# A hybrid decoder trunk: one step of the written-out order moved by a place on TensorE (twice), VectorE and GpSimd

## The chip, the cores and the metric

One core of one Trainium2 chip runs the whole program. The metric is the device time of one execution in microseconds (us).

## What is computed

The program takes 512 tokens of width 1024 through two decoder layers, after 16 learned meta tokens have been put in front (528 tokens; the 16 are dropped at the end). A layer is

```python
a = rms_norm(h, attn_norm)
proj = a @ w_in                     # columns parted among three head groups
o_a = dsa_attention(...)            # an indexer's scores choose 128 keys of each query, then softmax
o_b = forgetting_attention(...)     # softmax with q.k + cumsum(log_f) differences
o_c = gla_chunked(...)              # gated linear attention
h = h + concat(o_a, o_b, o_c) @ w_out
f = rms_norm(h, ffn_norm)
h = h + (silu(f @ w_gate) * (f @ w_up)) @ w_down
```

The four queries and keys of the first two groups are RMS-normed over each head of 64 features. All products are float32.

## The kernel before

**Products.** A float32 product is made of three: the weight is rounded to a high part (`whi`, ScalarE, L1702), the remainder is `wlo = raw - whi` (GpSimd, L888), the activations are split likewise (`xhi`, `xlo`), and TensorE adds `whi*xhi` (L1115), `whi*xlo` (L1116) and `wlo*xhi` (L1121) in one PSUM bank.

**Input projection.** `w_in` is cut into 24 units of 128 columns: unit 6 and 7 are the FoX queries, 8 and 9 the FoX keys, 10 and 11 the FoX values. A unit's 528 tokens are two halves of 264 (query units of layer 1: one of 512). A half is one PSUM bank and three pieces on TensorE, `("proj", unit, half, piece)`: pieces 0 and 1 are eight matmuls each with `whi`, piece 2 eight matmuls with `wlo`. VectorE then evicts the bank to `feat`, times the row's 1/rms (L2251, "eviction"). Three banks go round: the half three places later in the projection's order waits on TensorE for this eviction. ScalarE's and GpSimd's step `("proj", k, 1, 2)` rounds, or makes the remainder of, unit k + 2, since a buffer of two units is kept; the remainder's count (`split_done`) releases both piece 2 of that unit and the load of unit k + 4 on the DMA queue.

**The mixers between.** Everything else of the mixers is laid between these pieces. Steps that bear on the change:

- `norm(k)`, head norm of unit k: ScalarE squares the tile (L1772, L1773), GpSimd splits the squares (`sq_parts`, L982), TensorE sums them over the head with a block of ones (L1136) into a ring of four further banks, ScalarE takes the reciprocal root (L1742, L1783), and VectorE multiplies tile by gain by root (L2261).
- `split_q(n)`: ScalarE's high part (L1799) and VectorE's remainder (L2300) of half a query tile; numbers 4 to 7 are the sparse attention's four query heads. `logits(0, i, hd)` on TensorE (L1193) waits for `split_q(4 + hd)` on VectorE, and VectorE then adds the mask and takes the minimum (L2443) and frees the bank.
- `fox_log` and `spread_sums`: the forget gate's logarithm (ScalarE), its running sum (VectorE, L2345), and four copies of it into the rows of `k_fox` (GpSimd, L955): the "gate sums".
- `gate(t)`: two matmuls of the linear attention's gate (L1181).
- `index(i, hd)`: an indexer tile (TensorE L1193; ScalarE's relu L1894; VectorE's sum L2381).
- `topk`: rounds of maximum and replacement on VectorE (L2392, L2393).

**What sets the order.** Each engine runs its own list in order. The lists are written out by hand as strings in `STEPS_OF` (L258), one string for each layer and engine; a letter is a chain of steps, and each occurrence takes the next step of that chain that the engine has a part in (`ordered`, L315). A is the projection, D the norms, X the logits, Q GpSimd's clears (`masks`, `clear_fox`, `spread_sums`, ...). Banks of the ring follow from the order of the ring's jobs on TensorE (`BANKS_OF`, `Places`). Engines meet only at semaphores, so a list decides both what an engine does next and what it stands behind. A norm's matmuls, for example, wait like this (L1124):

```python
if k in SPLIT_SQUARES:
    pe.wait_ge(ev.sq_split, SPLIT_SQUARES.index(k) + 1)
```

and the first logit tiles of the sparse attention like this (L1204):

```python
pe.wait_ge(ev.key_split, 4)
pe.wait_ge(ev.query_split, 4 + hd + 1)
```

After the mixers each layer has its output projection and feed-forward on TensorE, which the change doesn't touch.

Of the kernel before, what the change touches and what calls it, by code (L numbers as in the profile page):

```python
# [115 lines left out]
PE, ACTE, DVEE, POOLE, DMAE = "PE", "ACT", "DVE", "POOL", "DMA"  # L116
# [120 lines left out]
class Places:  # L237
# [5 lines left out]
    def take(self, job, at):  # L243
# [12 lines left out]


STEPS_OF = (  # L258
    {PE: "AAAAAAAAAAAABAAADAAAAAAAFAAAAALAAAAAAAAADAMAAMDAAMMMMMMAAMAMAAADAAAAAADAPAAAAAAAAPAAXAXAAXADXAAALAaA"
     "LAAbAdDAAAAAXAXAXXAXXAaAXAAYXYbMAXMAAAAAadMAMAZYZXYAXZYXZAYXbAAAAdZYXZAZYAAXLAPAZRAARPALYXAYAXMaAMab"  # L260
     "AAAdLZZYAXYXZZbYAXYdZAAYAZZXXYXAYALXATSRSaAAATRTRSSATTaZbYXAdZADAZYAXYXDZYXAZbAYdDZAAAAYaZDYZAXXZAAX"
     "bAYdAXAYXaZYXZYXZYXZbYadZYZYZfZbfdfff",
     ACTE: "ABCADAPALHIHACIADCIMIMDMMMMMMCAMMDAJCODIPIAJAPCXIIXDCXXALaPLADeJJXAXXXXAaXYYMMAXXXaMMYXeYYYAXPXeAYXK"
     "YLXPAPLYXYXMaaMLeYYXYXYAXeXYYXALTYXaTATXTXTCYUaeCXDYAXYDYCUDeCXXYYDYaXXAUXeYXYaUYXXYXVXYVYVYVYAeae",
     DVEE: "AAAAADAFAAAPIAHAHIADMMIIDMMMMMMAAFNADANAOANDANANIAIXNIXAXINNXDNNAANNNcNANDNNNNXXXAXXAXPXAeXPAMMMAMcN"
     "XANNPXANXNPAXcXNAePeXXNARANRXNAMMXNMMcANNeNAXXNcNXeNANXNXXNXNSSRNRNARSSANNcNXNeNANXDXNAUDXcNNeDNANND"
     "XXAcAXXeUAXUXUVXVVXcVWWWWece",
     POOLE: "AAQAQAAACACAQAACQACAAQAAAQAAAACACCCAAA",
     DMAE: "AEEEAGAAEAEAGAAAAAAAAAAAAAAAAAA"},
    {PE: "AAAAAAAAABDAAAAAAAFAAAAALAADAMMAMDAAMMMAMMAADMAMAAAADAAAAADXXAAAXAAYYXAMAAAAAMaAMAAADAAMALALAAXAAAPA"  # L270
     "PAZYZAYXAXAAAAAZAYXAAAaZYAAAXbLAZYAAXAZYXZYAXAZbYXAAMAaRAARALMAPAAPALLASTSARATRASTSdRATZYXTZYXZYAXZY"
     "bXdADAadZZYYXADXZYZbXYAXZYXaZYXZDAZYAYXdbXZYXZaZYYdXZbXYdZXYaZXYZXZYXYbDZYZYZaZdbfdffff",
     ACTE: "BCAADAAHIICLADIHMMCMAIDMMMMMCADMMCPADICIAIIDAXXOXYAYJJXMaMJCMADJMALLAPPXAPYYXXYAXaYLAXYPYXXYXKYMAaLM"
     "APPXALLTATTUeTYYTYCXXYeXACDaXeYYUXDYYXAXCaYUXYDXYCXYUXYeXaYXeYXVeYXVXaYAYXYXYXDYVYVaee",
     DVEE: "AADAAFAAAIHIDAIMMHMIDMMAMMFANMDNAADIIXIXIDXAAAXMMONMNNANMNANDNNNANANNPNXANNNNNANANAXPAXPXANAPNcPXNXX"
     "NXAPMAMAMXNNRRANMANNANNNSNNSRNNRNNScARSeNXNNXNNXXANceNXeDUNAXXDcNUXXNXNNDNAXcXUUXeVVXecXWeXVXXXcWDVW"
     "Wcee",
     POOLE: "QQAAAAAACACACAAQQCAQAAAAAAQAAAACACCAAC",
     DMAE: "AEEEAGAAEAEAGAAAAAAAAAAAAAAAAAA"},
)  # L280
# [2737 lines left out]
```

## Time and profile before

| | |
|---|---|
| three runs | 1248.36, 1248.59 (median), 1249.31 us |
| profiled execution | span 1246.9 us from first to last instruction; the median of the runs is 1.7 us more |
| TensorE busy | 1232.7 us, 99% of the span |
| VectorE, ScalarE, GpSimd busy | 1025.6, 699.0, 171.2 us |
| granted TensorE clock | 1.000 on average |

The profile is of one execution, in microseconds from the start of its span. PE is TensorE, DVE VectorE, ACT ScalarE, POOL GpSimd. A timeline row gives start and duration, and where the engine stood idle before it, how long, and what released it. A matmul's row is longer than its step to the next, since matmuls overlap. Layer 0's mixers run from the start to some 238 us, layer 1's from about 640 to 860 us.

### The profile page before, as it was taken

The page shows a single profiled execution, that of the slowest core. Times are in us where ns is not written, and L with a number is a line of the kernel's source. Part 1 is how long each engine was busy: PE and PEld are TensorE (multiplying, and loading weights), DVE is VectorE, ACT ScalarE, POOL GpSimd, SP SyncE. Part 2 cuts the span into 40 slices and gives each one's busy share as a digit, 9 for nine tenths or more (in the row PEclk, how much of TensorE's full clock was granted, in tenths as well). Part 3 has the DMA queues.
Part 4 walks back from the last instruction along what each step waited for, and adds up shares of the span by engine and source line. Part 5 has one row for each costly group of instructions (what it writes and reads, how often), then busy time and mean ns, then how long its engine had stood idle before and what let it go on. Part 6 is the DMA issues. An engine that isn't in the chain of part 4 may idle for free.

```text
span 1246.9 us, 23723 instructions
## 1 busy us (share of the span) xinstructions
PE 1232.7 (99%) x9336; PEld 1181.9 (95%) x9336; DVE 1025.6 (82%) x1692; ACT 699.0 (56%) x1158; POOL 171.2 (14%) x120
## 2 busy tenths in 40 slices
PE   7999999999999999999999999999999999999999
PEld 7999999999999999999998899988899999998998
DVE  5797789588999999897665888894989999989865
ACT  6675547656555555753355765395665555558332
POOL 2564213100000000000033553121000000000000
PEclk9999999999999999999999999999999999999999
DMA  5322111132322222233323221110422332212333
GB/s 198 103 73 86 52 35 35 35 135 71 133 103 102 102 102 69 85 100 118 105 89 102 92 85 53 52 35 18 135 102 102 129 109 102 102 69 85 119 119 119
DMA packets 27387, 114.01 MB, mean 91 GB/s; under 512 B 3472, under 2 KB 4112, under 8 KB 21904
## 3 DMA queue, kind: packets, MB, share of 16 engines
q1 hardware_dynamic: 26560, 111.45, 26.9%
q8 instruction: 73, 1.20, 0.4%
q10 hardware_dynamic: 720, 1.09, 0.2%
q14 instruction: 34, 0.28, 0.1%
HBM read 108.79 MB, written 2.10 MB: 89 GB/s over the span
## 4 chain that ended last, share of the span: by engine, by line
PE 94%; DVE 3%; ACT 1%; issue 1%; POOL 1%; DMA 0%; SPq 0%; DVEq 0%; ACTq 0%; POOLq 0%
PE ps L1404 22%; PE ps L1410 11%; PE ps L1019 11%; PE ps L1115 6%; PE ps L1121 6%; PE ps L1116 6%; PE ps L1025 5%; PE ps L1488 5%; PE ps L1524 4%; PE ps L1245 3%; PE ps L1493 2%; PE ps L1529 2%; PE ps L1193 2%; PE ps L1218 2%; PE ps L1228 1%
## 5 line engine op out<-in xcount | busy, mean ns | idle before, releaser
L1115 PE MATMUL ps<-xhi,whi 128*128 128x264 f32 (+1 forms) x616 | 174.0, 310 | 1.3 <-DVE feat L2251 1.3
L1116 PE MATMUL ps<-xlo,whi 128*128 128x264 f32 (+1 forms) x616 | 167.5, 300 | 0.0
L888 POOL TENSOR_TENSOR wlo<-raw,whi 128x1024 fp32r<-128x1024 f32 x48 | 119.1, 2483 | 181.6 <-ACT whi L1702 181.0
L1115 PEld LDWEIGHTS ps<-xhi,whi 128*128 128x128 f32 x616 | 116.1, 188 | 5.9 <-DVE feat L2251 1.5
L1116 PEld LDWEIGHTS ps<-xlo,whi 128*128 128x128 f32 x616 | 116.2, 189 | 3.6
L1702 ACT ACTIVATE whi<-raw 128x1024 fp32r<-128x1024 f32 x74 | 77.9, 1054 | 55.0 <-PE ps L1025 30.6
L1121 PE MATMUL ps<-xhi,wlo 128*128 128x264 f32 (+1 forms) x616 | 100.5, 305 | 0.8 <-POOL wlo L888 0.8
L1121 PEld LDWEIGHTS ps<-xhi,wlo 128*128 128x128 f32 x616 | 85.3, 188 | 5.1 <-POOL wlo L888 1.2
L1404 PE MATMUL ps<-fhi,hi_a 128*128 128x264 f32 (+1 forms) x352 | 88.2, 283 | 0.0
L1404 PE MATMUL ps<-flo,hi_a 128*128 128x264 f32 (+1 forms) x352 | 88.1, 282 | 0.0
L1404 PE MATMUL ps<-flo,hi_b 128*128 128x264 f32 (+1 forms) x320 | 80.3, 283 | 0.0
L1404 PE MATMUL ps<-fhi,hi_b 128*128 128x264 f32 (+1 forms) x320 | 80.2, 282 | 0.0
L2027 ACT ACTIVATE w_part<-ps 128x264 f32<-128x264 f32 (+1 forms) x42 | 16.3, 387 | 91.1 <-PE ps L1410 91.1
L2138 ACT ACTIVATE whi<-raw 128x1024 fp32r<-128x1024 f32 (+2 forms) x42 | 38.4, 913 | 50.5 <-PE ps L1493 29.8
L1404 PE MATMUL ps<-xlo,hi_a 128*128 128x264 f32 (+1 forms) x264 | 66.5, 284 | 0.0
L1404 PE MATMUL ps<-xhi,hi_a 128*128 128x264 f32 (+1 forms) x264 | 66.3, 283 | 0.0
L1404 PEld LDWEIGHTS ps<-flo,hi_a 128*128 128x128 f32 x352 | 66.3, 188 | 0.0
L1404 PEld LDWEIGHTS ps<-fhi,hi_a 128*128 128x128 f32 x352 | 66.2, 188 | 0.0
L2251 DVE TENSOR_TENSOR feat<-ps,rstd 128x264 f32<-128x264 f32 (+1 forms) x84 | 38.4, 466 | 26.7 <-PE ps L1121 17.2
L1404 PEld LDWEIGHTS ps<-fhi,hi_b 128*128 128x128 f32 x320 | 60.3, 188 | 0.0
L2027 ACT ACTIVATE s<-ps 128x264 f32<-128x264 f32 (+1 forms) x84 | 32.5, 387 | 49.5 <-PE ps L1410 49.5
L1404 PEld LDWEIGHTS ps<-flo,hi_b 128*128 128x128 f32 x320 | 60.3, 188 | 0.0
(376 smaller groups left out, 3871.9 us busy)
## 6 DMA issues: line engine op xcount, KB each, us to landing
raw<-in_weights SPq DMA_DIRECT2D x116, 512.0 KB, 3.5
raw<-in_groups SPq DMA_DIRECT2D x42, 1024.0 KB, 4.8
out_hT<-h SPq DMA_DIRECT2D x7, 256.0 KB, 4.9
h<-in_hT SPq DMA_DIRECT2D x4, 264.0 KB, 6.3
h<-in_hT ACTq DMA_DIRECT2D x4, 264.0 KB, 6.0
cst<-in_consts SPq DMA_DIRECT2D x1, 780.5 KB, 9.0
xnb<-feat SPq DMA_DIRECT2D x10, 66.5 KB, 2.1
feat<-xnb SPq DMA_DIRECT2D x10, 66.5 KB, 2.1
```

The costliest lines, as they stand in the source:

```text
L888: nc.gpsimd.tensor_tensor(wlo[:, b], raw[:, b], whi[:, b].bitcast(F32), ALU.subtract).then_inc(split_done, 1)
L1019: nc.tensor.matmul(bank(bank_no, cut.stop - cut.start), whi[:, b, k % KT], x(k)[t][:, cut], start=(first and k == ks[0] and t == 0), stop= ...
L1025: ins = nc.tensor.matmul(bank(bank_no, cut.stop - cut.start), wlo[:, b, k % KT], x(k)[0][:, cut], start=False, stop=(last and k == ks[-1]))
L1115: nc.tensor.matmul(o, whi[:, k % 2, n], xhi[:, n, cut], start=(n == 0), stop=False)
L1116: nc.tensor.matmul(o, whi[:, k % 2, n], xlo[:, n, cut], start=False, stop=False)
L1121: ins = nc.tensor.matmul(o, wlo[:, k % 2, n], xhi[:, n, cut], start=False, stop=(n == KT - 1))
L1404: nc.tensor.matmul(bank(bank_no, width), high[:, of], x(i)[t], start=(begins and i == 0 and t == 0), stop=False, skip_group_check=True)
L1410: ins = nc.tensor.matmul(bank(bank_no, width), low, x, start=False, stop=(n == PAIRS - 1), skip_group_check=True)
L1488: nc.tensor.matmul(to, whi[:, slot, k], hidden_tiles(k0 + k)[t][:, cut], start=(begins and k == 0 and t == 0), stop=False, skip_group_chec ...
L1524: nc.tensor.matmul(down_bank(l, bank_no), high(i), x(i)[t], start=(begins and i == 0 and t == 0), stop=False, skip_group_check=True)
L1702: return nc.scalar.activation(whi[:, b], raw[:, b], ACT.Copy).then_inc(hi_done, 1)
L2027: nc.scalar.activation(to, bank(group_banks(n)[bank_name], width), ACT.Copy).then_inc(sv.snapped, 1)
```

## The change

Four letters move by a place or three; nothing else changes (further lines of the diff only shift the indentation of the strings). No instruction is added or taken away, and the order of the ring's jobs stays, so the banks do too.

| layer, engine | before | after |
|---|---|---|
| 0, TensorE | `norm 7`, `proj 8,1,2`, `gate 0` | `proj 8,1,2`, `norm 7`, `gate 0` |
| 0, GpSimd | `spread_sums`, remainder of unit 10, remainder of unit 11 | remainder of unit 10, `spread_sums`, remainder of unit 11 |
| 1, TensorE | `proj 9,1,0`, `norm 8`, `logits 0,1,0`, `logits 0,1,1`, `proj 9,1,1`, `proj 9,1,2` | `proj 9,1,0`, `proj 9,1,1`, `norm 8`, `logits 0,1,0`, `logits 0,1,1`, `proj 9,1,2` |
| 1, VectorE | `split_q 7`, `norm 8`, `logits 0,1,2`, eviction of 9,0, eviction of 9,1 | `split_q 7`, eviction of 9,0, `norm 8`, `logits 0,1,2`, eviction of 9,1 |

```diff
 STEPS_OF = (
-    {PE: "AAAAAAAAAAAABAAADAAAAAAAFAAAAALAAAAAAAAADAMAAMDAAMMMMMMAAMAMAAADAAAAAADAPAAAAAAAAPAAXAXAAXADXAAALAaA"
+    {PE: "AAAAAAAAAAAABAAADAAAAAAAFAAAAALAAAAAAAAADAMAAMDAAMMMMMMAAMAMAAADAAAAAAADPAAAAAAAAPAAXAXAAXADXAAALAaA"
...
-     POOLE: "AAQAQAAACACAQAACQACAAQAAAQAAAACACCCAAA",
+     POOLE: "AAQAQAAACACAAQACQACAAQAAAQAAAACACCCAAA",
...
-    {PE: "AAAAAAAAABDAAAAAAAFAAAAALAADAMMAMDAAMMMAMMAADMAMAAAADAAAAADXXAAAXAAYYXAMAAAAAMaAMAAADAAMALALAAXAAAPA"
+    {PE: "AAAAAAAAABDAAAAAAAFAAAAALAADAMMAMDAAMMMAMMAADMAMAAAADAAAAAADXXAAXAAYYXAMAAAAAMaAMAAADAAMALALAAXAAAPA"
...
-     DVEE: "AADAAFAAAIHIDAIMMHMIDMMAMMFANMDNAADIIXIXIDXAAAXMMONMNNANMNANDNNNANANNPNXANNNNNANANAXPAXPXANAPNcPXNXX"
+     DVEE: "AADAAFAAAIHIDAIMMHMIDMMAMMFANMDNAADIIXIXIADXAAXMMONMNNANMNANDNNNANANNPNXANNNNNANANAXPAXPXANAPNcPXNXX"
```

## Rows read from the trace of the kernel before

**Rows 1.** The page, part 1: busy time, share of the span and instructions by engine.

```profile
PE 1232.7 (99%) x9336; PEld 1181.9 (95%) x9336; DVE 1025.6 (82%) x1692; ACT 699.0 (56%) x1158; POOL 171.2 (14%) x120
```

**Rows 2.** The waits of TensorE: line, releaser, us in total, times, longest.

```profile
PE ps L1115 <- DVE feat L2251: 1.3, 1, 1.3
PE ps L1121 <- POOL wlo L888: 0.8, 1, 0.8
```

**Rows 3.** Timeline, layer 0, TensorE: start, duration, line, tiles, count, [idle before, releaser].

```profile
69.67 0.28 PE L1116 MATMUL ps<-xlo,whi 128*128 128x264 f32 x1
70.03 0.73 PE L1136 MATMUL ps<-sq_parts,ones_r 128*128 128x266 f32 x4
70.60 1.15 PE L1121 MATMUL ps<-xhi,wlo 128*128 128x264 f32 x8
71.58 0.41 PE L1181 MATMUL ps<-lr_parts,w_parts 80*128 80x266 f32 x2
...
80.82 1.24 PE L1121 MATMUL ps<-xhi,wlo 128*128 128x264 f32 x8 [0.75 <-POOL wlo L888]
...
82.86 0.20 PE L1193 MATMUL ps<-kk,mix_hi 128*16 128x16 f32 x2
...
84.31 0.20 PE L1193 MATMUL ps<-kk,q_tables 128*16 128x16 f32 x2 [0.17 <-DVE q_tables L2300]
```

**Rows 4.** Timeline, layer 0, GpSimd.

```profile
68.54 1.34 POOL L982 TENSOR_TENSOR sq_parts<-sqb,sq_parts 128x532 fp32r<-128x532 f32 x1 [2.76 <-ACT sq_parts L1773]
...
75.19 3.12 POOL L955 COPY k_fox<-feat 4x532 f32<-4x532 f32 x4 [2.89 <-DVE feat L2345]
78.39 5.20 POOL L888 TENSOR_TENSOR wlo<-raw,whi 128x1024 fp32r<-128x1024 f32 x2
```

**Rows 5.** Timeline, layer 0, ScalarE.

```profile
71.31 0.70 ACT L1742 ACTIVATE rnb<-ps,cst 128x532 f32<-128x532 f32 x1
...
74.51 1.06 ACT L1702 ACTIVATE whi<-raw 128x1024 fp32r<-128x1024 f32 x1
...
77.91 1.06 ACT L1702 ACTIVATE whi<-raw 128x1024 fp32r<-128x1024 f32 x1
```

**Rows 6.** Timeline, layer 0, VectorE.

```profile
76.36 0.77 DVE L2261 SCALAR_TENSOR_TENSOR feat<-feat,par_all,rnb 128x532 f32<-128x532 f32 x1
...
79.88 1.45 DVE L2300 TENSOR_TENSOR mix_hi<-feat,mix_hi 64x528 fp32r<-64x528 f32 x1
...
82.55 1.61 DVE L2300 TENSOR_TENSOR q_tables<-feat,q_tables 64x528 fp32r<-64x528 f32 x1
```

**Rows 7.** Timeline, layer 1, TensorE.

```profile
702.22 0.28 PE L1116 MATMUL ps<-xlo,whi 128*128 128x264 f32 x1
702.88 0.75 PE L1136 MATMUL ps<-sq_parts,ones_r 128*128 128x266 f32 x4 [0.38 <-POOL sq_parts L982]
...
710.92 0.39 PE L1115 MATMUL ps<-xhi,whi 128*128 128x264 f32 x1 [1.33 <-DVE feat L2251]
...
712.01 0.53 PE L1193 MATMUL ps<-kk,mix_hi 128*128 128x400 f32 x2
```

**Rows 8.** Timeline, layer 1, VectorE.

```profile
707.24 2.93 DVE L2261 SCALAR_TENSOR_TENSOR feat<-feat,par_all,rnb 128x532 f32<-128x532 f32 x1
710.20 0.31 DVE L2443 CUSTOM_DVE_ANT_0 probs<-ps,score 128x144 f32<-128x144 f32 x1
...
710.44 1.11 DVE L2251 TENSOR_TENSOR feat<-ps,rstd 128x264 f32<-128x264 f32 x3
```

**Rows 9.** Timeline, layer 1, GpSimd.

```profile
707.21 2.39 POOL L888 TENSOR_TENSOR wlo<-raw,whi 128x1024 fp32r<-128x1024 f32 x1 [1.65 <-ACT whi L1702]
```

**Rows 10.** Timeline, the start, TensorE.

```profile
6.92 0.59 PE L1019 MATMUL ps<-xhi,whi 128*128 128x264 f32 x1 [6.92 <-ACT whi L1702]
...
11.59 0.42 PE L1019 MATMUL ps<-xhi,whi 128*128 128x264 f32 x1
11.81 0.42 PE L1019 MATMUL ps<-xlo,whi 128*128 128x264 f32 x1
```

More of the change, by code:

```diff
@@ L258 @@
 STEPS_OF = (
-    {PE: "AAAAAAAAAAAABAAADAAAAAAAFAAAAALAAAAAAAAADAMAAMDAAMMMMMMAAMAMAAADAAAAAADAPAAAAAAAAPAAXAXAAXADXAAALAaA"
-     "LAAbAdDAAAAAXAXAXXAXXAaAXAAYXYbMAXMAAAAAadMAMAZYZXYAXZYXZAYXbAAAAdZYXZAZYAAXLAPAZRAARPALYXAYAXMaAMab"
-     "AAAdLZZYAXYXZZbYAXYdZAAYAZZXXYXAYALXATSRSaAAATRTRSSATTaZbYXAdZADAZYAXYXDZYXAZbAYdDZAAAAYaZDYZAXXZAAX"
-     "bAYdAXAYXaZYXZYXZYXZbYadZYZYZfZbfdfff",
+    {PE: "AAAAAAAAAAAABAAADAAAAAAAFAAAAALAAAAAAAAADAMAAMDAAMMMMMMAAMAMAAADAAAAAAADPAAAAAAAAPAAXAXAAXADXAAALAaA"
+         "LAAbAdDAAAAAXAXAXXAXXAaAXAAYXYbMAXMAAAAAadMAMAZYZXYAXZYXZAYXbAAAAdZYXZAZYAAXLAPAZRAARPALYXAYAXMaAMab"
+         "AAAdLZZYAXYXZZbYAXYdZAAYAZZXXYXAYALXATSRSaAAATRTRSSATTaZbYXAdZADAZYAXYXDZYXAZbAYdDZAAAAYaZDYZAXXZAAX"
+         "bAYdAXAYXaZYXZYXZYXZbYadZYZYZfZbfdfff",
@@ L263 @@
      ACTE: "ABCADAPALHIHACIADCIMIMDMMMMMMCAMMDAJCODIPIAJAPCXIIXDCXXALaPLADeJJXAXXXXAaXYYMMAXXXaMMYXeYYYAXPXeAYXK"
-     "YLXPAPLYXYXMaaMLeYYXYXYAXeXYYXALTYXaTATXTXTCYUaeCXDYAXYDYCUDeCXXYYDYaXXAUXeYXYaUYXXYXVXYVYVYVYAeae",
+           "YLXPAPLYXYXMaaMLeYYXYXYAXeXYYXALTYXaTATXTXTCYUaeCXDYAXYDYCUDeCXXYYDYaXXAUXeYXYaUYXXYXVXYVYVYVYAeae",
      DVEE: "AAAAADAFAAAPIAHAHIADMMIIDMMMMMMAAFNADANAOANDANANIAIXNIXAXINNXDNNAANNNcNANDNNNNXXXAXXAXPXAeXPAMMMAMcN"
-     "XANNPXANXNPAXcXNAePeXXNARANRXNAMMXNMMcANNeNAXXNcNXeNANXNXXNXNSSRNRNARSSANNcNXNeNANXDXNAUDXcNNeDNANND"
@@ L267 @@
-     "XXAcAXXeUAXUXUVXVVXcVWWWWece",
-     POOLE: "AAQAQAAACACAQAACQACAAQAAAQAAAACACCCAAA",
+           "XANNPXANXNPAXcXNAePeXXNARANRXNAMMXNMMcANNeNAXXNcNXeNANXNXXNXNSSRNRNARSSANNcNXNeNANXDXNAUDXcNNeDNANND"
+           "XXAcAXXeUAXUXUVXVVXcVWWWWece",
+     POOLE: "AAQAQAAACACAAQACQACAAQAAAQAAAACACCCAAA",
      DMAE: "AEEEAGAAEAEAGAAAAAAAAAAAAAAAAAA"},
-    {PE: "AAAAAAAAABDAAAAAAAFAAAAALAADAMMAMDAAMMMAMMAADMAMAAAADAAAAADXXAAAXAAYYXAMAAAAAMaAMAAADAAMALALAAXAAAPA"
-     "PAZYZAYXAXAAAAAZAYXAAAaZYAAAXbLAZYAAXAZYXZYAXAZbYXAAMAaRAARALMAPAAPALLASTSARATRASTSdRATZYXTZYXZYAXZY"
-     "bXdADAadZZYYXADXZYZbXYAXZYXaZYXZDAZYAYXdbXZYXZaZYYdXZbXYdZXYaZXYZXZYXYbDZYZYZaZdbfdffff",
+    {PE: "AAAAAAAAABDAAAAAAAFAAAAALAADAMMAMDAAMMMAMMAADMAMAAAADAAAAAADXXAAXAAYYXAMAAAAAMaAMAAADAAMALALAAXAAAPA"
+         "PAZYZAYXAXAAAAAZAYXAAAaZYAAAXbLAZYAAXAZYXZYAXAZbYXAAMAaRAARALMAPAAPALLASTSARATRASTSdRATZYXTZYXZYAXZY"
+         "bXdADAadZZYYXADXZYZbXYAXZYXaZYXZDAZYAYXdbXZYXZaZYYdXZbXYdZXYaZXYZXZYXYbDZYZYZaZdbfdffff",
@@ L273 @@
      ACTE: "BCAADAAHIICLADIHMMCMAIDMMMMMCADMMCPADICIAIIDAXXOXYAYJJXMaMJCMADJMALLAPPXAPYYXXYAXaYLAXYPYXXYXKYMAaLM"
-     "APPXALLTATTUeTYYTYCXXYeXACDaXeYYUXDYYXAXCaYUXYDXYCXYUXYeXaYXeYXVeYXVXaYAYXYXYXDYVYVaee",
-     DVEE: "AADAAFAAAIHIDAIMMHMIDMMAMMFANMDNAADIIXIXIDXAAAXMMONMNNANMNANDNNNANANNPNXANNNNNANANAXPAXPXANAPNcPXNXX"
-     "NXAPMAMAMXNNRRANMANNANNNSNNSRNNRNNScARSeNXNNXNNXXANceNXeDUNAXXDcNUXXNXNNDNAXcXUUXeVVXecXWeXVXXXcWDVW"
-     "Wcee",
+           "APPXALLTATTUeTYYTYCXXYeXACDaXeYYUXDYYXAXCaYUXYDXYCXYUXYeXaYXeYXVeYXVXaYAYXYXYXDYVYVaee",
@@ L278 @@
+     DVEE: "AADAAFAAAIHIDAIMMHMIDMMAMMFANMDNAADIIXIXIADXAAXMMONMNNANMNANDNNNANANNPNXANNNNNANANAXPAXPXANAPNcPXNXX"
+           "NXAPMAMAMXNNRRANMANNANNNSNNSRNNRNNScARSeNXNNXNNXXANceNXeDUNAXXDcNUXXNXNNDNAXcXUUXeVVXecXWeXVXXXcWDVW"
+           "Wcee",
      POOLE: "QQAAAAAACACACAAQQCAQAAAAAAQAAAACACCAAC",
```

## The prediction, made before the changed kernel was run

> **What bounds the kernel now.** First the page's busy shares: TensorE is busy 99% of the span, VectorE 82% [rows 1]. So the sum is about TensorE's gaps alone: whatever is taken from a gap there is gained at the end, and whatever is added is lost, as no later stretch has slack to take it up. Then the waits of TensorE: after the wait at the start, its two longest are 1.3 us for an eviction and 0.8 us for a weight's remainder [rows 2], one in each place that the change touches. Then the timelines of those two places, engine by engine, for what each gap waits on and, above all, for what is next in line once it closes. The largest that could be hoped for is the sum of the gaps, some 3 us or 0.24%; 0.2% (2.5 us) is about what a measurement of this kernel can tell from no change.
>
> **Layer 0, TensorE.** Pieces of eight matmuls take 0.98 us (70.60 to 71.58), a step of 0.12. The last matmul before norm 7 starts at 69.67, so the norm could follow at 69.79; it starts at 70.03, when its squares are split (GpSimd, 68.54 + 1.34 = 69.88) [rows 3, 4]. With the piece put ahead, it fills that gap: 0.24 gained, and the norm's sums start at 69.79 + 0.98 = 70.77, ending 0.73 later at 71.50.
>
> **Layer 0, GpSimd.** The remainder of unit 10 now goes ahead of the gate sums, which took 75.19 to 78.31. Before, it ended at 80.8 and TensorE waited 0.75 for it [rows 3, 4]. It needs its rounding, which ended at 74.51 + 1.06 = 75.57. ScalarE is busy on norm 7 from 71.31 [rows 5]; that norm's sums now end at 71.50, and I take 0.1 from there to ScalarE, so all up to this rounding moves 0.29 later. It ends at 75.86, and GpSimd starts at about 76.0 (0.07 to 0.15 behind the rounding: 707.21 in layer 1). With 2.39 for a remainder [rows 9] it ends at 78.4, and TensorE wants it at 80.82 - 0.75 - 0.24 = 79.8. That wait goes: 0.75, with 0.24 together 1.0 us.
>
> **What is late next in layer 0.** In layer 1 VectorE's norm multiply L2261 is issued at 707.24, just behind a remainder of GpSimd that started at 707.21. It takes 2.93 in place of 0.77 and ends at 710.17, which is 0.57 after GpSimd (709.60) [rows 6, 8, 9]. So of the two, the one that starts second stands until the other is done. In layer 0 norm 7's multiply is at 76.36 and met no remainder before; now it falls 0.36 behind the start of unit 10's. It ends at 78.4 + 0.57 = 78.97 instead of 77.13: 1.84 late. VectorE goes in order, and so do the evictions and the two rounds of top-k behind it; the remainder of query head 0 (L2300, 79.88) comes at 81.72 [rows 6].
>
> The Trainium skill, page "SBUF — State Buffer", section "Who interferes with whom", has this as a rule: a VectorE instruction with two SBUF inputs and a GpSimd instruction that reads SBUF shut each other out, and the first keeps the ports for the whole instruction. By its word "fully blocks" the multiply would start only at GpSimd's end and take its 0.77, 0.20 more than the row's 0.57. Three such ends follow one another below, so by the rule's word the sum would be 0.6 worse. I go by the row.
>
> GpSimd meanwhile: gate sums from 78.5 for about 3.1 (one of the four copies held up by the multiply, as before), to 81.6, then the remainder of unit 11. That unit's rounding (77.91, behind norm 7's multiply on ScalarE's list) moves 1.84 too and ends at 80.8, in time [rows 4, 5]. So at 81.6 to 81.7 GpSimd's remainder and VectorE's query remainder meet, each able to hold the other.
>
> - GpSimd first, the likelier, as it leads by up to 0.1 and a lead of 0.03 was enough at 707.21: head 0's remainder ends at 81.6 + 2.39 + 0.57 = 84.56. TensorE's first logit tile needs it and goes 0.15 later (from 82.55 + 1.61 = 84.16 to 84.31 in the rows), at 84.7 instead of 82.86; it stands some 3 us. Next GpSimd's squares L982 (1.34) slip in and end at 85.8, so head 1's remainder ends at 86.35 and the second tile starts at 86.5 instead of 84.31 [rows 3, 4, 6]: **2.2 us lost**, the 1.0 of gain eaten in it.
> - VectorE first: head 0 is through at 82.4, unit 11's remainder runs from 82.3 to 84.7, head 1's ends at 85.3 and the second tile starts at 85.4: 1.1 us lost.
>
> Behind that, TensorE, VectorE and GpSimd are all shifted alike. The gate sums are wanted only by the second group's logits, many pieces later; the loads on the DMA queue hang on the remainders, unit 12's moves forward with unit 10's, unit 13's hardly moves, and neither is read for several pieces. Nothing for these.
>
> **Layer 1, TensorE.** Norm 8 could start at 702.22 + 0.12 = 702.34 and starts at 702.88 [rows 7]: the piece put ahead fills 0.54. ScalarE and GpSimd behind the norm are bound by other work there, so 0.54 is gained at the start of the next piece.
>
> **Layer 1, VectorE.** The eviction of 9,0 came behind norm 8's multiply (to 710.17) and the logit tile (710.20), at 710.5, and TensorE stood 1.33 to 710.92 for it [rows 7, 8]. Ahead of the norm it is done at 707.6, while TensorE wants the bank at 709.05. So 1.33 goes. The multiply then starts at 707.6, still behind the same remainder, and ends at the same 710.17; the logit tile still frees its bank at 710.51, and indexer tile (3,2) takes this bank. It came 1.09 behind 710.92, now at 709.05 + 1.09 = 710.14, and so waits until about 710.56: 0.42 back. Sum 0.54 + 1.33 - 0.42 = **1.45 gained**. Unit 12's remainder, some 12 us on, has its gate sums and squares moved by 0.3 to 1.4 only, which can cost 0 to 0.25; I take 1.4. Evictions of 9,1 and 10,0 keep their time or come earlier.
>
> **Sum.** 2.2 lost, 1.4 gained: 0.8 slower. The profiled span is 1246.9, which becomes 1247.7; the median of the runs stands 1.7 over the span, so 1249.4.
>
> **Rivals.**
> - *VectorE wins the meeting* at 81.7. For it: my starts are good to about 0.1 only. 1.1 - 1.4 = -0.3: 1248.3. Within 0.2% like the forecast.
> - *The multiply is not shut out*: unit 10's remainder starts after 76.36, so GpSimd waits for the multiply (0.77) and not it for GpSimd. The remainder ends at 79.5, still in time, and everything hoped for comes: layer 0 gains 1.0, layer 1 gains 1.4, 1246.2. Against it: the rounding would have to be 0.35 later than I have it. The change not doing what it says, in that the piece ahead fills nothing, is part of this only in name: lists are followed in order, so I give that none.
> - *TensorE slows after its stand* (slower). In the first case it stands 3 us at the first logit tile. At the start it stands 6.92 and then runs with a step of 0.22 instead of 0.12 [rows 3, 10], to 11.81 at least (about 5 us), which is what the lower of the two levels (1.2 against 2.4 GHz) would look like, though the mean granted clock of the whole span is given as 1.000. The price is 5 / 0.22 = 23 matmuls at 0.10: 2.3 us, so 0.8 + 2.3 = 3.1 slower, 1251.7. Against it: after the 1.33 at 710.92 the step is the usual one (1.09 for eight matmuls and their start [rows 7]); no row stands 3 us in the middle, so it decides from somewhere between 1.33 and 6.92. The Trainium skill, page "TensorE: Matmul & The Clock Gate", section "Why this matters for your kernels", warns of TensorE gaps between bursts in the middle of a kernel for this; the trace bears it out only for the start.
>
> **Chances.** Forecast (GpSimd first) 0.53, VectorE first 0.22, not shut out 0.12, slower clock 0.07, anything else 0.06. Faster by over 0.2% needs all the hoped gain and a little more than 2.4, half of "not shut out" and some of the rest: 0.09. Slower by over 0.2% needs the clock, or a further collision in layer 0 (the copies of the clears against heads 2 and 3, at most 0.3) with layer 1's gain missing: 0.12. Within 0.2%: 0.79. The range takes in the first two cases with 0.3 to 0.6 for their bounds and the spread of the runs (0.95): 1247.4 to 1250.8. It leaves out the cases at either end.
>
> **What would show it.** Right: no wait of TensorE for `wlo` near 80 and none for `feat` near 709; in their place TensorE waiting at L1193 for VectorE's L2300 (`mix_hi`, then `q_tables`) at 82 to 86 for some 3 us and 0.7; L2261 at 76.4 taking about 2.6; a wait of 0.4 at the indexer tile near 710. VectorE first: 1 us and then 1.7 at L1193. Wrong: L2261 at 0.77 there, no wait at L1193, and TensorE's gaps in layer 0 shorter than before; or matmuls with a step of 0.22 behind the stand.

## The result, and the profile after

The changed kernel takes 1250.94 us (median of 15 runs, 1250.58 to 1252.04) against 1248.65 (15 runs, 1248.2 to 1249.56): a ratio of 1.0019, 95% interval 1.0012 to 1.0026. It is 2.3 us slower; the forecast was 0.8 us slower. Its profiled execution spans 1249.1 us and took 1250.89.

First the page's busy times and the waits of TensorE, as in [rows 1, 2].

```profile
PE 1234.6 (99%) x9336; PEld 1183.7 (95%) x9336; DVE 1028.4 (82%) x1692; ACT 699.1 (56%) x1158; POOL 171.1 (14%) x120
```

```profile
PE ps L1193 <- DVE mix_hi L2300: 2.8, 1, 2.8
...
PE ps L1193 <- DVE stat L2443: 0.4, 1, 0.4
```

Both waits of [rows 2] are gone, 2.1 us together. One of 2.8 us at the first logit tile of layer 0 stands in their place, and a small one in layer 1. But the waits do not tell it all: TensorE is also *busy* 1.9 us longer with the same 9336 matmuls, so something made matmuls slower. Next the timeline of TensorE, at the start, in layer 0, in layer 1 and at the end, and the rows of before that the forecast did not need, for comparison (before first, then after).

```profile
24.44 1.14 PE L1121 MATMUL ps<-xhi,wlo 128*128 128x264 f32 x8
...
88.07 1.21 PE L1121 MATMUL ps<-xhi,wlo 128*128 128x264 f32 x8
...
716.28 1.14 PE L1121 MATMUL ps<-xhi,wlo 128*128 128x264 f32 x8
...
1242.70 1.10 PE L1493 MATMUL ps<-hhi,wlo 128*128 128x256 f32 x8
```

```profile
24.77 1.15 PE L1121 MATMUL ps<-xhi,wlo 128*128 128x264 f32 x8
...
79.94 1.13 PE L1121 MATMUL ps<-xhi,wlo 128*128 128x264 f32 x8
...
84.88 0.20 PE L1193 MATMUL ps<-kk,mix_hi 128*16 128x16 f32 x2 [2.84 <-DVE mix_hi L2300]
...
85.24 0.42 PE L1116 MATMUL ps<-xlo,whi 128*128 128x264 f32 x1
85.46 0.42 PE L1115 MATMUL ps<-xhi,whi 128*128 128x264 f32 x1
...
86.78 0.24 PE L1193 MATMUL ps<-kk,q_tables 128*16 128x16 f32 x2
86.87 1.92 PE L1121 MATMUL ps<-xhi,wlo 128*128 128x264 f32 x8
88.63 0.28 PE L1115 MATMUL ps<-xhi,whi 128*128 128x264 f32 x1
88.75 0.29 PE L1116 MATMUL ps<-xlo,whi 128*128 128x264 f32 x1
...
91.26 1.23 PE L1121 MATMUL ps<-xhi,wlo 128*128 128x264 f32 x8
...
713.71 0.63 PE L1193 MATMUL ps<-kk,mix_hi 128*128 128x400 f32 x2 [0.41 <-DVE stat L2443]
...
718.10 1.14 PE L1121 MATMUL ps<-xhi,wlo 128*128 128x264 f32 x8
...
1244.91 1.10 PE L1493 MATMUL ps<-hhi,wlo 128*128 128x256 f32 x8
```

The same matmuls, after less before: +0.33 at 24.77 (nothing has changed yet there; the start differs so from execution to execution), +3.19 at 91.26, +1.82 at 718.10, +2.21 at 1244.91. (Right ahead of the change, at 66.84 before and 67.22 after, the shift is 0.38, so what follows is good to about 0.05.) So **layer 0 lost 2.86, layer 1 gained 1.37 and gave 0.39 of it back further down** (0.98 net), and the change is worth +1.88 in these two executions. In layer 0 the stand is 2.84 long and the second tile comes at 86.78, which is 2.14 later than [rows 3] once the start's 0.33 is taken off. From there to 91.26 another 0.72 goes: between 85.24 and 88.63 matmuls of 264 columns take steps of 0.22, and 0.12 again from 88.63 on. The stretches of 1 us show why (columns: length of the stretch, busy time and instructions of TensorE, its weight loads, VectorE, ScalarE, GpSimd, then the granted TensorE clock, then DMA):

```profile
84.00:85.00 1.00, 0.12 (x3) 0.15 (x3) 0.97 (x2) 0.00 (x0) 1.00 (x2) 1.00 0.00 0
85.00:86.00 1.00, 1.00 (x7) 1.00 (x6) 0.97 (x2) 0.00 (x0) 0.92 (x1) 0.50 0.81 98
86.00:87.00 1.00, 1.00 (x8) 0.92 (x7) 0.97 (x4) 0.28 (x2) 0.97 (x1) 0.50 0.97 393
87.00:88.00 1.00, 1.00 (x6) 1.00 (x6) 0.89 (x4) 0.98 (x3) 0.88 (x3) 0.50 0.09 33
88.00:89.00 1.00, 1.00 (x9) 1.00 (x8) 0.71 (x4) 0.53 (x2) 0.85 (x1) 0.79 0.00 0
89.00:90.00 1.00, 1.00 (x12) 0.98 (x11) 0.42 (x3) 0.00 (x0) 0.00 (x0) 1.00 0.07 16
```

The granted clock, 1.00 through the stand, is 0.50 (the lower of its two levels, 1.2 GHz) from 85 to 88 and part of 88 to 89: 3 x 0.50 + 0.21 = 1.71 us of clock are missing. Before, the same stretches all read 1.00.

What VectorE and GpSimd did (their timelines, VectorE first):

```profile
76.74 2.46 DVE L2261 SCALAR_TENSOR_TENSOR feat<-feat,par_all,rnb 128x532 f32<-128x532 f32 x1
...
81.95 2.79 DVE L2300 TENSOR_TENSOR mix_hi<-feat,mix_hi 64x528 fp32r<-64x528 f32 x1
...
85.23 1.25 DVE L2300 TENSOR_TENSOR q_tables<-feat,q_tables 64x528 fp32r<-64x528 f32 x1
...
710.43 0.43 DVE L2251 TENSOR_TENSOR feat<-ps,rstd 128x264 f32<-128x264 f32 x1
710.78 2.52 DVE L2261 SCALAR_TENSOR_TENSOR feat<-feat,par_all,rnb 128x532 f32<-128x532 f32 x1
```

```profile
76.23 2.40 POOL L888 TENSOR_TENSOR wlo<-raw,whi 128x1024 fp32r<-128x1024 f32 x1 [3.54 <-ACT whi L1702]
78.69 3.06 POOL L955 COPY k_fox<-feat 4x532 f32<-4x532 f32 x4
81.83 2.34 POOL L888 TENSOR_TENSOR wlo<-raw,whi 128x1024 fp32r<-128x1024 f32 x1
...
718.23 2.92 POOL L955 COPY k_fox<-feat 4x532 f32<-4x532 f32 x4 [5.50 <-DVE feat L2345]
...
723.64 1.34 POOL L982 TENSOR_TENSOR sq_parts<-sqb,sq_parts 128x532 fp32r<-128x532 f32 x1
724.93 2.76 POOL L888 TENSOR_TENSOR wlo<-raw,whi 128x1024 fp32r<-128x1024 f32 x1
```

Unit 10's remainder starts at 76.23 and norm 7's multiply at 76.74, where it takes 2.46 for the 0.77 of [rows 6]. Then the remainder of unit 11 starts at 81.83 and head 0's remainder 0.12 later: it takes 2.79 and ends at 84.74, 0.57 after GpSimd (84.17). That is the forecast's chain on these two engines, to 0.2 us (less the start's shift) at every link. No semaphore stands between the two: the multiply was issued and its inputs were there. So engines do not meet at semaphores alone, as the description of the lists has it; VectorE and GpSimd also hold each other up directly, and no list shows that.

### The profile page after: what moved, and what is told of

Read it like the earlier page. It is cut to its first block, busy times and chain, and to the rows that moved or that the text cites. A ratio compares the mean times of both kernels' runs of the same rounds, so it can differ in the third digit from the quotient of the medians.

```text
span 1249.1 us, 23723 instructions
## 1 busy us (share of the span) xinstructions
PE 1234.6 (99%) x9336; PEld 1183.7 (95%) x9336; DVE 1028.4 (82%) x1692; ACT 699.1 (56%) x1158; POOL 171.1 (14%) x120
## 4 chain that ended last, share of the span: by engine, by line
PE 96%; DVE 3%; issue 1%; DMA 0%; ACT 0%; SPq 0%; DVEq 0%; ACTq 0%
PE ps L1404 22%; PE ps L1410 11%; PE ps L1019 11%; PE ps L1115 6%; PE ps L1121 6%; PE ps L1116 6%; PE ps L1025 5%; PE ps L1488 5%; PE ps L1524 4%; PE ps L1245 3%; PE ps L1493 2%; PE ps L1529 2%; PE ps L1193 2%; PE ps L1218 2%; PE ps L1228 1%; PE ps L1302 1%
```

## The experiments

Kernels that ran together share the runs of the kernel before: 28 runs (median 1248.47) beside `l0_only`, `l1_only`, `norm_first` and `query_first`, 33 (1248.51) beside `l0_pe_only`, `l0_pool_only`, `filled` and `tiles_later`, 27 (1248.44) beside `combined`, `l1_dve_only` and `l1_pe_only`. Diffs are against the kernel before where one part of the change is tried, else against the changed kernel. The clock is the mean granted one of an execution; all runs of the kernel before have 1.000.

### Layer 0 alone, layer 1 alone

`l0_only`:

```diff
-{PE: "AAAAAAAAAAAABAAADAAAAAAAFAAAAALAAAAAAAAADAMAAMDAAMMMMMMAAMAMAAADAAAAAADAPAAAAAAAAPAAXAXAAXADXAAALAaA"
+{PE: "AAAAAAAAAAAABAAADAAAAAAAFAAAAALAAAAAAAAADAMAAMDAAMMMMMMAAMAMAAADAAAAAAADPAAAAAAAAPAAXAXAAXADXAAALAaA"
...
-POOLE: "AAQAQAAACACAQAACQACAAQAAAQAAAACACCCAAA",
+POOLE: "AAQAQAAACACAAQACQACAAQAAAQAAAACACCCAAA",
```

> Layer 0's two moves alone, layer 1 as before. Theory (unit 10's remainder shuts out norm 7's multiply, the query remainder comes late, TensorE stands 2.8 us at the first logit tile and then runs at half the clock for some 3.4 us): 2.6 to 3.0 us slower than before, a granted clock of 0.5 behind the stand, mean clock under 1. Rival (layer 0 is harmless, the loss is in layer 1): within 0.4 us of before. Rival (the stand costs, the low clock is chance): 1.9 us slower with a clock of 1.000 in some looks.

Measured: 1251.93 (6 runs, 1251.45 to 1253.23), ratio 1.0031 (1.0019 to 1.0043): 3.5 slower, more than the 2.6 to 3.0 that were expected. Its profile has the stand of 2.84 at the first tile, and every one of its runs has a clock of 0.997 to 0.999. The six runs fall in two groups: three with 0.999 took 1251.45 to 1251.65, three with 0.997 took 1252.2 to 1253.23, and the profiled one is of the first group.

`l1_only`:

```diff
-{PE: "AAAAAAAAABDAAAAAAAFAAAAALAADAMMAMDAAMMMAMMAADMAMAAAADAAAAADXXAAAXAAYYXAMAAAAAMaAMAAADAAMALALAAXAAAPA"
+{PE: "AAAAAAAAABDAAAAAAAFAAAAALAADAMMAMDAAMMMAMMAADMAMAAAADAAAAAADXXAAXAAYYXAMAAAAAMaAMAAADAAMALALAAXAAAPA"
...
-DVEE: "AADAAFAAAIHIDAIMMHMIDMMAMMFANMDNAADIIXIXIDXAAAXMMONMNNANMNANDNNNANANNPNXANNNNNANANAXPAXPXANAPNcPXNXX"
+DVEE: "AADAAFAAAIHIDAIMMHMIDMMAMMFANMDNAADIIXIXIADXAAXMMONMNNANMNANDNNNANANNPNXANNNNNANANAXPAXPXANAPNcPXNXX"
```

> Layer 1's two moves alone, layer 0 as before. Theory: 0.9 us faster (1.4 gained by the twelfth projection unit, 0.4 of it given back there), clock 1.000, a wait of 0.4 at the indexer tile. Rival (layer 1 gives all of it back, or is the loss): no change, or slower.

Measured: 1247.84 (11 runs, 1246.84 to 1248.72), ratio 0.9996 (0.9987 to 1.0005), clock 1.000 in all. By its timeline, less the 0.11 that it is ahead before layer 1's change, 1.39 is gained at the piece behind the eviction and 0.98 at the end. The medians give 0.6, with an interval that takes in no change; the sign rests on the timeline. So the loss is layer 0's alone, and what layer 1 brings does not cover it.

### Which move of layer 0

`l0_pe_only`:

```diff
-{PE: "AAAAAAAAAAAABAAADAAAAAAAFAAAAALAAAAAAAAADAMAAMDAAMMMMMMAAMAMAAADAAAAAADAPAAAAAAAAPAAXAXAAXADXAAALAaA"
+{PE: "AAAAAAAAAAAABAAADAAAAAAAFAAAAALAAAAAAAAADAMAAMDAAMMMMMMAAMAMAAADAAAAAAADPAAAAAAAAPAAXAXAAXADXAAALAaA"
```

> Layer 0's move on TensorE alone: norm 7 one piece later, GpSimd in the order of before. Theory: 0.24 gained ahead of the norm and lost again at the wait for unit 10's remainder, which grows from 0.75 to 1.0; no change, within 0.2 us. Rival (the norm's delay is what makes the multiply late): slower by 1 us or more, with a stand at the logit tile.

Measured: 1248.53 (11 runs, 1248.08 to 1249.14), ratio 0.9999 (0.999 to 1.0008), clock 1.000. The 0.24 gained ahead of the norm is lost again at the weight's remainder, whose wait grows from 0.75 [rows 3] to 1.11.

`l0_pool_only`:

```diff
-POOLE: "AAQAQAAACACAQAACQACAAQAAAQAAAACACCCAAA",
+POOLE: "AAQAQAAACACAAQACQACAAQAAAQAAAACACCCAAA",
```

> Layer 0's move on GpSimd alone: unit 10's remainder ahead of the gate sums, the norm on TensorE where it was. Theory (this move alone makes the collision): the multiply of norm 7 takes 2.3, the first logit tile stands about 2.3 us, the clock falls in some runs; 2.0 to 2.8 us slower than before. Rival (it needs the norm's delay too): the multiply takes 0.77 and the kernel is 0.5 to 1 us faster than before.

Measured: 1251.34 (11 runs, 1249.86 to 1252.0), ratio 1.0021 (1.0012 to 1.003): 2.8 slower, with a stand of 2.31 and a multiply of 2.25. The clock is 0.998 or 0.999 in nine runs; the two at 1.000 took 1249.86 and 1250.19, the nine 1251.15 to 1252.0. GpSimd's move does the damage alone.

### Undoing the collision

`norm_first`: norm 7's multiply goes ahead of a round of top-k on VectorE, so that it starts before the remainder.

```diff
-DVEE: "AAAAADAFAAAPIAHAHIADMMIIDMMMMMMAAFNADANAOANDANANIAIXNIXAXINNXDNNAANNNcNANDNNNNXXXAXXAXPXAeXPAMMMAMcN"
+DVEE: "AAAAADAFAAAPIAHAHIADMMIIDMMMMMMAAFNADANAOADNANANIAIXNIXAXINNXDNNAANNNcNANDNNNNXXXAXXAXPXAeXPAMMMAMcN"
```

> The whole change, and in layer 0 VectorE does norm 7's multiply ahead of a round of top-k instead of behind it. Theory: the multiply then starts ahead of unit 10's remainder and takes its 0.77; the first logit tile waits 0.3 us at most; the second may still wait for unit 11's remainder, until about 84.4; no low clock. Layer 0 is between 0 and 1.6 us faster than before, with layer 1 in all 0.9 to 2.5 faster than before. Rival (the late gate sums or the late unit 11 are the loss, not the multiply): a stand of over 2 us at the first tile again, and 2 us slower.

Measured: 1246.40 (11 runs, 1246.22 to 1247.36), ratio 0.9985 (0.9976 to 0.9994), clock 1.000. **It is faster than both kernels**, 4.5 us below the changed one. Its timelines of VectorE, GpSimd and TensorE:

```profile
74.97 0.77 DVE L2261 SCALAR_TENSOR_TENSOR feat<-feat,par_all,rnb 128x532 f32<-128x532 f32 x1
...
79.50 1.12 DVE L2300 TENSOR_TENSOR mix_hi<-feat,mix_hi 64x528 fp32r<-64x528 f32 x1
...
81.11 0.70 DVE L2300 TENSOR_TENSOR q_tables<-feat,q_tables 64x528 fp32r<-64x528 f32 x1
```

```profile
75.47 2.53 POOL L888 TENSOR_TENSOR wlo<-raw,whi 128x1024 fp32r<-128x1024 f32 x1 [3.54 <-ACT whi L1702]
...
81.20 2.88 POOL L888 TENSOR_TENSOR wlo<-raw,whi 128x1024 fp32r<-128x1024 f32 x1
```

```profile
81.11 0.20 PE L1193 MATMUL ps<-kk,mix_hi 128*16 128x16 f32 x2
...
82.22 0.20 PE L1193 MATMUL ps<-kk,q_tables 128*16 128x16 f32 x2
...
84.79 0.20 PE L1193 MATMUL ps<-kk,mix_lo 128*16 128x16 f32 x2 [0.32 <-DVE mix_lo L2300]
```

Now the multiply is first, by 0.50, and takes its 0.77; the remainder behind it takes 2.53. At 81.11 head 1's remainder leads GpSimd by 0.09, takes its 0.70, and this time GpSimd is the one that pays (2.88 for 2.40). TensorE waits at neither of the first two tiles. So one letter in one list turns the loss into the gain that was hoped for, and the cause of the stand is that multiply's place.

`query_first`: the multiply stays where it is, but head 0's remainder goes ahead of a round of top-k.

```diff
-DVEE: "AAAAADAFAAAPIAHAHIADMMIIDMMMMMMAAFNADANAOANDANANIAIXNIXAXINNXDNNAANNNcNANDNNNNXXXAXXAXPXAeXPAMMMAMcN"
+DVEE: "AAAAADAFAAAPIAHAHIADMMIIDMMMMMMAAFNADANAOANDANAINAIXNIXAXINNXDNNAANNNcNANDNNNNXXXAXXAXPXAeXPAMMMAMcN"
```

> The whole change, and in layer 0 VectorE takes the first query remainder ahead of a round of top-k. Theory: the multiply is still shut out (some 2.4 us), but the query remainder now starts ahead of unit 11's remainder; the first tile waits under 0.6 us, the second some 2 us, until 84.7. If the clock falls only behind a stand as long as 2.8 us, it stays at 1.000, layer 0 loses 0.4 and the whole is 0.5 faster than before. Rival (the clock falls behind any stand of some 2 us): mean clock under 1, and some 1 us slower than that.

Measured: 1248.79 (11 runs, 1247.95 to 1249.78), ratio 1.0002 (0.9993 to 1.0011); 0.3 slower where 0.5 faster was expected. Head 0 is clear of the remainder (0.70), but head 1 is not: 1.98, and a stand of 2.21 at the second tile. Eight runs have a clock of 1.000 (1247.95 to 1248.89, middle 1248.58), three 0.998 or 0.999 (1249.48 to 1249.78). Those eight are level with before too, so the clock is not the whole miss: the second collision was priced too low. In the profile the second tile comes at 84.83, which is 0.71 later than [rows 3] with the start's shift of 0.19 put back, where a loss of 0.4 was expected. That is half of the 0.6 by which the eight miss; the rest is not placed.

`combined`: `norm_first`, with heads 0 and 1 ahead of a round of top-k as well (head 1 ahead of an eviction too).

```diff
-DVEE: "AAAAADAFAAAPIAHAHIADMMIIDMMMMMMAAFNADANAOANDANANIAIXNIXAXINNXDNNAANNNcNANDNNNNXXXAXXAXPXAeXPAMMMAMcN"
+DVEE: "AAAAADAFAAAPIAHAHIADMMIIDMMMMMMAAFNADANAOADNANAIINAXNIXAXINNXDNNAANNNcNANDNNNNXXXAXXAXPXAeXPAMMMAMcN"
```

> The changed kernel with norm 7's multiply ahead of a round of top-k (as in norm_first) and also head 0's and head 1's remainders ahead of one. My theory: norm_first has already taken every wait of TensorE for these tiles but 0.3 at the third, so that this gives 1246.4 within 0.3, clock 1.000. Rival: remainders that come earlier meet another GpSimd operation (the gate sums' copies) and hold it, and the remainder of unit 11 with it: a wait for wlo, 0.5 or more slower than norm_first.

Measured: 1246.26 (11 runs, 1245.91 to 1247.14), ratio 0.9983 (0.9974 to 0.9992). Level with `norm_first`, as expected. The rival's meeting is there (the gate sums' copies take 3.49 against 3.05 in `norm_first`), but TensorE does not wait for it.

### What the stand costs beside its length

`filled`: TensorE is kept at work in place of standing. Twenty matmuls are added ahead of the first tile, in its bank; the tile then overwrites what they leave. (Three lines are added, so line numbers below them are 3 higher.)

```diff
+if l == 0 and (i, hd) == (0, 0):
+    for _ in range(20):
+        nc.tensor.matmul(bank(b0, CUT), ones_r[:, 0:128], kk[:, 0, 0:CUT], start=True, stop=True)
```

> The whole change; ahead of layer 0's first logit tile TensorE runs 20 matmuls of 264 columns into the tile's own bank, about 2.4 us, which the tile then overwrites. Everything is as late as in the changed kernel, only TensorE no longer stands for 2.8 us but for 0.4. Theory (the stand costs 1.9 us in layer 0 by lateness, and what comes on top of it is the clock that falls behind it): mean clock 1.000 in every run, the second tile waits some 0.6, and the time is 1.0 us over before, 0.9 to 1.3 us under the changed kernel. Rival (the slower matmuls have another cause than the stand): clock under 1 again, and the time of the changed kernel.

Measured: 1249.75 (11 runs, 1249.02 to 1250.12), ratio 1.0006 (0.9997 to 1.0015), clock 1.000 in all eleven. TensorE's timeline:

```profile
24.66 1.14 PE L1121 MATMUL ps<-xhi,wlo 128*128 128x264 f32 x8
...
81.72 2.60 PE L1212 MATMUL ps<-kk,ones_r 128*128 128x264 f32 x20
84.68 0.21 PE L1193 MATMUL ps<-kk,mix_hi 128*16 128x16 f32 x2 [0.37 <-DVE mix_hi L2303]
...
86.52 0.20 PE L1193 MATMUL ps<-kk,q_tables 128*16 128x16 f32 x2 [0.54 <-DVE q_tables L2303]
...
90.26 1.23 PE L1121 MATMUL ps<-xhi,wlo 128*128 128x264 f32 x8
```

The remainders collide as in the changed kernel and the tiles come hardly sooner (84.68 and 86.52 against 84.88 and 86.78, of which 0.11 is the start), yet the matmuls run at full step, and 1.05 us of the loss are gone (1.24 slower than its runs of before, not 2.29; the slowest of its runs is under the fastest of the changed kernel, 1250.58). The matmul that came at 91.26 is at 90.26 here: 2.19 behind the 88.07 of before, 1.97 less the start's 0.22. So layer 0's 2.86 is **1.97 for the collisions and 0.89 for the clock** by the two timelines; by the medians the clock's share is 1.05. It is less than the 1.71 of missing clock, in the main because TensorE would have waited for the second tile anyway (0.54 here).

`tiles_later`: the four logit tiles and norm 8 go one to three pieces later on TensorE, for whom the late tiles then do not matter.

```diff
-{PE: "AAAAAAAAAAAABAAADAAAAAAAFAAAAALAAAAAAAAADAMAAMDAAMMMMMMAAMAMAAADAAAAAAADPAAAAAAAAPAAXAXAAXADXAAALAaA"
+{PE: "AAAAAAAAAAAABAAADAAAAAAAFAAAAALAAAAAAAAADAMAAMDAAMMMMMMAAMAMAAADAAAAAAADPAAAAAAAAPAAAAAXAXAXADXALAaA"
```

> The whole change, and on TensorE layer 0's four first logit tiles and norm 8 come one to three pieces later, so that pieces of the projection fill the stand. VectorE and GpSimd collide as before. Theory: the first tile waits 0.3 at most, the second 0.7, the third 0.8; no low clock; layer 0 is 0.3 faster than before, in all 1.3 faster than before (0.4 to 1.7). Rival (the lateness of the remainders is paid further down, by a wait of the later tiles or of the banks): the wait turns up behind the moved tiles and the time is that of the changed kernel.

Measured: 1248.87 (11 runs, 1248.35 to 1249.88), ratio 1.0002 (0.9993 to 1.0011), clock 1.000. Against the expectation of 1.3 faster this is a miss. The first tile no longer waits and the clock stays up, but new waits come up: 0.5 and 0.6 at the next two tiles, 0.7 for a weight's rounding, 0.5 for a softmax tile of ScalarE. Of the 2.29 of loss 1.9 are saved (0.36 slower than its runs of before): the clock's share and some 0.9 of the stand, but the lateness of VectorE is passed on to whoever needs it next, and nothing is left of layer 0's gain.

### The two moves of layer 1

`l1_dve_only`:

```diff
-DVEE: "AADAAFAAAIHIDAIMMHMIDMMAMMFANMDNAADIIXIXIDXAAAXMMONMNNANMNANDNNNANANNPNXANNNNNANANAXPAXPXANAPNcPXNXX"
+DVEE: "AADAAFAAAIHIDAIMMHMIDMMAMMFANMDNAADIIXIXIADXAAXMMONMNNANMNANDNNNANANNPNXANNNNNANANAXPAXPXANAPNcPXNXX"
```

> Layer 1's VectorE move alone: the eviction of 9,0 goes ahead of norm 8, TensorE's order stays as before, so norm 8's sums still wait for their squares. My theory: the wait of 1.33 for the eviction goes, the indexer tile gives back about 0.4 and unit 12's chain a part of the rest: 1.0 to 1.3 faster at the start of the next piece, 0.6 to 1.0 faster at the end (1247.5 to 1247.9 beside 1248.5), clock 1.000. Rival (the two moves of layer 1 need each other): without TensorE's move the time stands on norm 8 instead, and less than 0.4 is left.

Measured: 1247.88 (11 runs, 1247.14 to 1248.45), ratio 0.9995 (0.9986 to 1.0004), clock 1.000. By its timeline, less the 0.53 that it is ahead before layer 1's change, 1.35 is gained behind the eviction and 0.96 at the end: all of what `l1_only` has.

`l1_pe_only`:

```diff
-{PE: "AAAAAAAAABDAAAAAAAFAAAAALAADAMMAMDAAMMMAMMAADMAMAAAADAAAAADXXAAAXAAYYXAMAAAAAMaAMAAADAAMALALAAXAAAPA"
+{PE: "AAAAAAAAABDAAAAAAAFAAAAALAADAMMAMDAAMMMAMMAADMAMAAAADAAAAAADXXAAXAAYYXAMAAAAAMaAMAAADAAMALALAAXAAAPA"
```

> Layer 1's TensorE move alone: the piece of 9,1 fills the 0.54 ahead of norm 8, but the eviction of 9,0 still stands behind norm 8's multiply on VectorE, which ends when GpSimd's remainder ends. My theory: the wait for the eviction grows from 1.33 to about 1.9 and the time stays, within 0.2 of before, clock 1.000. Rival (the gap filled ahead of the norm is a gain of its own): 0.5 faster.

Measured: 1249.97 (11 runs, 1248.03 to 1250.56), ratio 1.0008 (0.9999 to 1.0017): 1.5 slower by the medians, with an interval that only just takes in no change, where none was expected. The first matmul behind the eviction, and the stretches of 1 us behind it (columns as above, the granted clock third from the end):

```profile
710.66 0.39 PE L1115 MATMUL ps<-xhi,whi 128*128 128x264 f32 x1 [1.78 <-DVE feat L2251]
```

```profile
711.00:712.00 1.00, 1.00 (x8) 1.00 (x7) 0.90 (x4) 0.53 (x3) 0.00 (x0) 0.69 0.89 356
712.00:713.00 1.00, 1.00 (x6) 0.99 (x5) 0.93 (x3) 0.00 (x0) 0.00 (x0) 0.50 0.20 78
713.00:714.00 1.00, 1.00 (x6) 1.00 (x6) 0.96 (x2) 0.00 (x0) 0.00 (x0) 0.50 0.00 0
714.00:715.00 1.00, 1.00 (x7) 1.00 (x7) 0.97 (x2) 0.00 (x0) 0.00 (x0) 0.60 0.00 0
```

The wait grew as expected, to 1.78, and then the clock falls, for 0.31 + 0.50 + 0.50 + 0.40 = 1.71 us as in the changed kernel. Eight runs have a clock below 1 (1249.62 to 1250.56, middle 1250.04), the other three 1248.03, 1248.09 and 1249.13. So the clock falls in a layer and behind a wait that have nothing to do with the first case: the stand does it, not what the logit tiles are. And here little of it is hidden: the matmul behind the stand comes at 710.66 against 710.92 before, but the piece of 716.28 at 717.52, so 1.50 of the 1.71 are lost there.

## Why the prediction was wrong

**Where it was right.** The likeliest case came about, link by link as far as the first logit tile. The piece ahead of norm 7 and the earlier remainder took away TensorE's waits. Norm 7's multiply fell behind unit 10's remainder and took 2.46 (forecast about 2.6). GpSimd won the meeting near 81.7, by 0.12. The first tile came 0.15 earlier than forecast and the second 0.05 earlier (84.88 and 86.78, less 0.33, against 84.7 and 86.5). For the second tile that is luck. The forecast had TensorE wait some 0.7 there, and the trace shows no wait: TensorE came to it late by itself, at the lower clock. In `filled`, at the full clock, the wait is 0.54 and the tile comes at 86.52 less 0.22, which is 0.2 earlier than forecast. The wait named for layer 1 appeared: 0.41 against 0.42 at the indexer tile. As for the Trainium skill, page "SBUF — State Buffer", section "Who interferes with whom": the runs agree that whoever is first keeps the other out, in both directions (`norm_first`), but the one kept out ends 0.57 after the other and not its full 0.70 or 0.77 later, twice more in the trace (79.20 behind 78.63, 84.74 behind 84.17). The row was the better guide. The page's "fully blocks" is said of VectorE's 2-port modes; of an instruction with two SBUF inputs, as here, it says that it contends. And what the prediction made of the rule was too much: 0.20 for each of three ends, 0.6, where the two query remainders (0.70 alone) would have come 0.13 later each, so 0.46.

**The step that failed: the sum had nothing for the clock, which had been made a rival with a chance of 0.07, and it fell in every run.** The argument against it was that "no row stands 3 us in the middle, so it decides from somewhere between 1.33 and 6.92." The forecast itself put the stand at some 3 us, well into that open stretch, and the mean clock of 1.000 was no argument: nothing in the middle of that kernel had stood so long, and the column does not cover the start, where it reads 1.00 from 7 to 12 us while matmuls take steps of 0.22 [rows 10]. The slow step behind the start's stand was the better sign. An even chance would have been fair. Put together, the longest stand in the middle (of the profiled execution; the others have no trace) against the clock:

| kernel | stand, us | runs with a clock below 1 |
|---|---|---|
| before; `l0_pe_only` | 1.33 | 0 of 15, 28, 33 and 27; 0 of 11 |
| `l1_pe_only` | 1.78 | 8 of 11 |
| `query_first` | 2.21 | 3 of 11 |
| `l0_pool_only` | 2.31 | 9 of 11 |
| after; `l0_only` | 2.84 | 15 of 15; 6 of 6 |
| `norm_first`, `combined`, `filled`, `tiles_later`, `l1_only`, `l1_dve_only` | below 1.33 | 0 of 11 each |

In these runs the first clock below 1 is met between 1.33 and 1.78. The middle of the table does not follow the length (8 of 11 at 1.78, 3 of 11 at 2.21). With eleven runs each that may be chance; whether something else decides as well was not tried and stays open. The Trainium skill, page "TensorE: Matmul & The Clock Gate", section "Why this matters for your kernels", warns of TensorE gaps between bursts in the middle of a kernel. These runs agree that such gaps cost the clock, but they show it behind shorter ones than the page sets as its bound: 1.78 us was enough in 8 of 11 runs.

**The price of that rival was off as well.** It took 5 us at the lower level from the start, 23 matmuls, 2.3 us. The stretch measured 3.4 us (85.24 to 88.63), and part of it lies in the wait for the second tile, so that it cost 0.89 by the timelines and 1.05 by the medians. So the rival's 1251.7 is 0.8 above the result, and the forecast's 1249.4 is 1.5 below it.

**Layer 1 was sized 0.4 too high.** 1.45 was forecast at the start and 1.37 came. Of it 0.39 was then given back, where "0 to 0.25" was allowed. GpSimd's timeline of before, for the rows of after above:

```profile
715.44 2.69 POOL L955 COPY k_fox<-feat 4x532 f32<-4x532 f32 x4 [5.84 <-DVE feat L2345]
...
721.33 1.34 POOL L982 TENSOR_TENSOR sq_parts<-sqb,sq_parts 128x532 fp32r<-128x532 f32 x1 [0.79 <-ACT sq_parts L1773]
722.64 2.73 POOL L888 TENSOR_TENSOR wlo<-raw,whi 128x1024 fp32r<-128x1024 f32 x1
```

And TensorE's weight loads (PEld) after the change, in a place where before it none waits for GpSimd:

```profile
727.75 0.30 PEld L1121 LDWEIGHTS ps<-xhi,wlo 128*128 128x128 f32 x2 [0.46 <-POOL wlo L888]
```

TensorE was ahead by 1.37 there, but VectorE was not: its multiply still ended with GpSimd's remainder, so the gate sums come 2.79 later than before while TensorE is 1.82 later. GpSimd, which had stood 0.79 ahead of unit 12's squares, now works through without a gap; the squares are 2.31 late and unit 12's remainder 2.29. TensorE does not wait for the squares, but the load of that remainder's first weight waits 0.46 for it, and TensorE ends at 2.21. That is read from the rows; no run took this chain away. The two moves of layer 1 also do not add up as the forecast had it: VectorE's is worth 1.35 alone, and TensorE's 0.54 only moved on to the next wait, and cost the clock where it stood alone.

**The sum as it should have been**, by the timelines: 1.97 for layer 0's collisions (forecast 2.2), 0.89 for the clock (forecast nothing), 0.98 gained in layer 1 (forecast 1.4): 1.88. The medians differ by 2.29, and the 0.4 between is not placed. The start, where the code is the same, came 0.33 later in the profiled execution of after than in that of before; and seven of the 15 runs had a lower mean clock than the profiled one (0.997 and 0.998 against 0.999) and took 1251.03 to 1252.04. Each may hold a part. One fall of 1.71 us is 0.14% of the span and reads as 0.999; a mean of 0.997 is at least 3.1 us of missing clock. So four of the runs (0.997, 1251.62 to 1252.04) lost more clock than the profiled one, and where they lost it no trace shows.

## What to carry to other kernels

When a step is moved forward to close a wait, look at which instruction of another engine it now starts just ahead of: an operation that locks another out can cost it most of its own length (2.40 us of GpSimd made the multiply 1.69 longer, 2.34 made head 0's remainder 2.09 longer), and the place of one letter (`norm_first`) decides who pays. Where a change makes TensorE stand for longer than any row of the trace shows it standing, give the lower clock an even chance and price it at the measured low stretch, less what a later wait hides. And an engine freed early gains only until the next thing it needs from an engine that was not.

## What was not expected of the hardware

- Stands of 1.78 to 2.84 us in the middle of a busy kernel bring the granted clock to 0.50, and not at once: TensorE resumes at 84.88 and reads 0.50 from 85 on in the changed kernel, but in `l1_pe_only` it resumes at 710.66 and the 0.69 of 711 to 712 puts the fall at about 711.4. What is missing is 1.71 us of clock in both, and also in `query_first` (0.13 + 3 x 0.50 + 0.08), `l0_only` and `l0_pool_only`. Below 2.84 it happens only in some runs of the same program.
- The lead that decides a meeting of VectorE and GpSimd was 0.12 and 0.09 us in these runs, and the loser of either kind waits: VectorE 2.79 for 0.70, GpSimd 2.88 for 2.40.
